# Hybrid transformer blocks, fp32, one core: a gate panel of HGRN ahead of the gated delta's scores, and the solver's `gd_x0` behind the panel of HGRN's values

## Chip, core and metric

The kernel runs on one core of a Trainium2 chip. The metric is the device time of one execution in microseconds. The kernel before takes 1782.95 us (median of three runs).

## What is computed

Two blocks follow one another on an input of 256 positions by 1024 channels, all in float32. The first has two layers of FFN, mixer, FFN; the second is one layer of retention, dilated attention, MLP and a gated embedding. The change is in the mixer of the first block, so it runs twice. The mixer projects the normed input with `w_in` and runs three parts side by side, HGRN2 (`hg_`), gated delta (`gd_`) and RG-LRU (`rg_`):

```python
def hybrid_mixer(h, lb, w_in, ...):
    proj = (h @ w_in)
    (hg_q, hg_f, hg_i, hg_g, gd_q, gd_k, gd_v, gd_z, gd_b, gd_a,
     rg_x, rg_gate) = jnp.split(proj, SPLIT_POINTS, axis=-1)
    o_hg = hgrn2_chunked(q, 1.0 - f, hg_i, jnp.log(f))
    o_hg = head_rmsnorm(o_hg, hg_norm_w) * jax.nn.silu(hg_g)
    o_gd = gated_delta_chunked(cq, ck, cv, g, beta)
    o_gd = head_rmsnorm(o_gd, gd_norm_w) * jax.nn.silu(gd_z)
    o_rg = rg_lru(xc, wr, br, wi, bi, lam) * jax.nn.gelu(rg_gate, approximate=True)
    return jnp.concatenate([o_hg, o_gd, o_rg], axis=-1) @ w_out

# inside gated_delta_chunked, for each chunk
    lower = jnp.where(strict, jnp.einsum('bhtd,bhsd->bhts', kb, ki) * decay, 0.0)
    sol = lax.linalg.triangular_solve(eye + lower, rhs, left_side=True, lower=True, unit_diagonal=True)
    scores = jnp.einsum('bhtd,bhsd->bhts', qi, ki) * decay
```

`hg_g` is columns 768 to 1023 of `w_in` (the gate panel that the change moves) and `hg_i` columns 512 to 767 (HGRN's values).

## The kernel before

All weights pass through the core once, in panels of 1 MB. SyncE loads a panel into one of three `raw` slots. ScalarE makes its high half `w_hi` (line 1526), VectorE the low half `w_lo` = raw - w_hi (line 2028), each with two slots, and TensorE multiplies high by high, high by low and low by high. A panel of 256 columns of `w_in` is 48 matmuls of 256 columns into one of three PSUM banks `colb` (c modulo 3), and ScalarE evacuates the bank with the activation of the panel (line 1636).

The order of all work is one list, `schedule`. The functions of `mixer` append panels (`cp`) and steps (`step`) to it, and each engine's program walks the whole list in that order, doing its own part of each entry. So moving one entry moves it on every engine. An entry has parts besides what it is named for:

- For ScalarE a panel entry first makes w_hi up to the next panel (`split_hi_to(p + 1)`), which waits for the raw data and for the end of the panel two before it; then it evacuates its own bank.
- For VectorE a panel entry makes w_lo up to the next panel (`split_lo_to(p + 1)`), which waits for that panel's w_hi. With `next_later` (the panel of hv) it goes only to its own. The steps in `AHEAD` (`spread` among them) also make w_lo one panel on.
- For TensorE a panel entry is its matmuls.

The steps around the change, with what each engine does: `spread` puts the gates on all partitions; its last part on ScalarE (line 1842) raises `gates_read`. `hg_exponents` n: VectorE builds differences of the cumulated log gates (lines 2389 and 2390), ScalarE takes their exponentials (line 1849). `gd_scores`: TensorE, once `gates_read` is there, makes 32 products k k' and k q' of 128x128 into the four `acc` banks; VectorE scales eq (2327), then for each of two chunks masks (2331), scales (2338) and adds the identity (2341), which raises `gd_x`, then makes sc (2343). `gd_x0`: TensorE multiplies the solver's first matrices by the identity, 32 small matmuls; ScalarE copies them out (1859) and resets a buffer (1853). `hg_first`: VectorE, two products (2396, 2397). `rg_end`: VectorE, the scan of RG-LRU and its gate (2316 to 2321). Then the solver's loop, i = 1 to 6: `gd_y` (TensorE; VectorE's masked copy at line 2352), `hg_level` (TensorE and VectorE) and `gd_z` (TensorE; ScalarE copies at 1879).

Line 917 is the helper through which nearly all matmuls go, so they are told apart by their tiles.

Of the kernel before, what the change touches and what calls it, by code (L numbers as in the profile page):

```python
# [26 lines left out]
PC = 256  # L27
# [87 lines left out]
def build(nc, ap, out, stop_at=None):  # L115
    ctx = ExitStack()
    with ctx:
# [57 lines left out]
        def view(at, *shape):  # L175
            n = int(np.prod(shape))
            v = arena[:, at:at + n]
            if len(shape) == 2:
                v = v.rearrange("p (a b) -> p a b", b=shape[1])
            if len(shape) == 3:  # L180
                v = v.rearrange("p (a b c) -> p a b c", b=shape[1], c=shape[2])
            return v
# [23 lines left out]
        hf, hq, hgate = view(A2, 2, T), view(A2 + 512, 2, T), view(A2 + 1024, 2, T)  # L206
# [74 lines left out]
        def panel(src, kt, ncols, kind, xop, ready, **more):  # L281
            nonlocal n_col, n_act, n_dve, n_row
            r = dict(p=len(panels), src=src, kt=kt, nc=ncols, kind=kind, xop=xop, ready=ready, **more)
            if kind != "row" and early[0]:
                n_scaled[0] += 1
                r.update(xop=g_op(early[1]["ops"]), ready=[], gained=count["fill"] if early[0] == EARLY else None, scaled=n_scaled[0],
                         norm=count["norm"], fill=early[1], half=EARLY - early[0])
                early[0] -= 1
                fresh[0] = True
            elif kind != "row":  # L290
                r["fresh"], fresh[0] = fresh[0], False
            if kind != "row":
                r["c"] = n_col
                n_col += 1
                if r["by"] == "act":
                    n_act += 1
                    r["n"] = n_act
                else:
                    n_dve += 1
                    r["n"] = n_dve  # L300
                bank_users.append((r["by"], r["n"]))
            else:
                n_row += 1
            panels.append(r)
            schedule.append(("panel", r))
            return r
# [33 lines left out]
        def step(name, **more):  # L340
            schedule.append((name, dict(panel=len(panels), nx=count["x"], op=len(ops), **more)))
# [21 lines left out]
        def pre_norm(gain, at):  # L363


            step("gained", gain=gain, at=at, n=count["fill"] + 1)
            n = norm_sum("x", "fill", gain=gain, at=at)
            f = fill(norm=n, gain=gain, at=at)
            return f

        def x_update(kind, **more):
            count["x"] += 1
            step("x_update", kind=kind, group=count["group"], first=0, **more)
            if kind in ("half", "whole"):
                acc_reader[0] = ("x_updated", 4 * count["x"])
            if kind == "post":
                count["normed"] += 1
                acc_reader[0] = ("acc_normed", 4 * count["normed"])

        def operand(src, ready):  # L380

            r = dict(r=len(ops), src=src, ready=ready)
            ops.append(r)
            return r
# [7 lines left out]
        def kpn(w):  # L392
            return w.rearrange("(k p) n -> p k n", p=P)

        def row_gemm_panel(w, i, r, first, last, base=None, woven=False, by_token=False):
            if r is not None:
                ready = [("op_ready", r["r"] + 1)]
                r["panel"] = len(panels)
                get = op_tiles(r)
            else:  # L400
                ready = base[0]
                get = (lambda kk, i=i: base[1](2 * i + kk))
            if first and acc_reader[0]:
                ready = ready + [acc_reader[0]]
            p = panel(kpn(w)[:, 2 * i:2 * i + 2, :], 2, D, "row", get, ready, first=first, last=last, woven=woven, by_token=by_token)
            if last:
                count["group"] += 1
            return p
# [51 lines left out]
        def mixer(l):  # L460
            f = pre_norm("norm_mix", KD * l)
            w = kpn(ap["w_in"][l])
            ready = [("u_ready", 4 * f)]

            def cp(c0, n, kind, evac, by="act", **more):
                return panel(w[:, :, c0:c0 + n], KD, n, kind, u_op, ready, by=by, evac=evac, **more)["n"]

            def y_operand(i, ready):
                r = operand(u32[:, 2 * i:2 * i + 2, :].rearrange("p a b -> p (a b)"), [ready])
                step("op_hi", r=r)  # L470
                step("op_lo", r=r)
                return r

            def gd_panel(i, **more):
                return cp(1024 + i * PC, PC, "A",
                          ("tap", gd_in[:, 2 * i:2 * i + 2, 3:], qkv[:, 2 * i:2 * i + 2, :], 48 * l + 36 + 2 * i), **more)


            b = cp(RGX0, PC, "A", ("copy", rg_in[:, :, 3:], 0))
            e = gd_panel(0)  # L480
            step("rg_conv", l=l, evac=b)
            for i in range(1, 6):
                n = gd_panel(i, split_first=i == 1)
                if i == 1:
                    cp(GATES0, P, "A", ("copy", gt[0], 0, 8), by="dve")
                    step("gate_rows", l=l)
                step("gd_conv", l=l, i=i - 1, evac=e)
                e = n
            cp(2560, PC, "A", ("silu", z[:, 0:2, :]))
            step("gd_conv", l=l, i=5, evac=e)  # L490
            step("gate_log", l=l)
            step("gate_cum", l=l)
            step("gd_ss", l=l)
            f = cp(256, PC, "A", ("sigmoid", hf))
            step("rg_gates", l=l)
            step("gate_copies", l=l)
            e = cp(0, PC, "A", ("silu", hq))
            step("hg_log", l=l, evac=f)
            step("rg_scan", l=l)
            step("spread", l=l)  # L500
            step("hg_cum", l=l, evac=e)
            for n in range(3):
                step("hg_exponents", l=l, n=n)
            d = cp(RGX0 + PC, PC, "A", ("gelu", rgate))
            step("gd_scores", l=l)
            cp(768, PC, "A", ("silu", hgate))
            step("gd_x0", l=l)
            step("hg_first", l=l)
            e = cp(512, PC, "B", ("copy", hv, 0), next_later=True)
            step("rg_end", l=l, evac=d)  # L510

            n = 0
            for i in range(1, 7):
                step("gd_y", l=l, i=i)
                for half in range(2):
                    if n < 9 and (half == 0 or i <= 3):
                        step("hg_level", l=l, n=n, evac=e)
                        n += 1
                    if half == 0:
                        step("gd_z", l=l, i=i)  # L520
                    if n <= 9 and (half == 0 or i <= 3) and n + 2 < 8:
                        step("hg_exponents", l=l, n=n + 2)
                if i == 1:
                    y_rg = operand(u32[:, 6:8, :].rearrange("p a b -> p (a b)"), [("rg_y", l + 1)])
                    step("op_hi", r=y_rg)
                if i == 4:
                    step("op_lo", r=y_rg)
            acc_reader[0] = ("gd_solved", 2 * l + 2)
            woven = row_gemm_panel(ap["w_out"][l], 3, y_rg, True, False, woven=True)
            step("hg_out", l=l, woven=woven)  # L530
            step("gd_chunks", l=l)
            y_hg = y_operand(0, ("hg_y", l + 1))
            step("gd_norm", l=l)
            row_gemm_panel(ap["w_out"][l], 0, y_hg, False, False)
            tail_c[l] = n_col
            ready = [("gd_orstd", 2 * l + 1)]
            step("gd_out", l=l, i=0)
            y_gd = y_operand(1, ("gd_out", 2 * l + 1))
            e = cp(2560 + PC, PC, "A", ("silu", z[:, 2:4, :]))
            step("gd_out", l=l, i=1, evac=e)  # L540
            row_gemm_panel(ap["w_out"][l], 1, y_gd, False, False)
            y_gd = y_operand(2, ("gd_out", 2 * l + 2))
            row_gemm_panel(ap["w_out"][l], 2, y_gd, False, True)
            x_update("whole")
# [2127 lines left out]
```

How the kernel before makes its waits and increments, by code:

```python
        def first_ready(eng, part, p, b):  # L732
            if b < 3:
                eng.wait_ge(sem(f"first_{part}"), 3 * p + b + 1)
            else:
                eng.wait_ge(sem(f"w_{part}_ready"), p + 1)
# [8 lines left out]
        def evacuated(eng, n):  # L746
            by, done = bank_users[n]
            eng.wait_ge(sem(f"{by}_evac"), done)
# [1 line left out]
        def col_bank_free(eng, n):  # L750
            evacuated(eng, n)
            both = [last_both[i] for i in (n, n + 1, n + 2) if i in last_both]
            if both:
                eng.wait_ge(sem("both_added"), both[-1])
# [1 line left out]
        def bank_done(eng, r, b):  # L757
            if b < 3:
                eng.wait_ge(sem("acc_bank"), 3 * (r["group"] - 1) + b + 1)
            else:
                eng.wait_ge(sem("panel_used"), r["panel"])
# [31 lines left out]
        @block.sync  # L794
# [4 lines left out]
            def load_quarter(b):  # L799
                dst = chunk_of(raw[:, 0, :], b).rearrange("p (k n) -> p k n", k=2)
                if b >= 2:
                    sp.wait_ge(sem(f"x_loaded{b - 2}"), 16)
                sp.dma_start(dst, panels[0]["src"][:, 2 * b:2 * b + 2, :]).then_inc(sem(FIRST_RAW[b][0]), 16)
# [8 lines left out]
                if what == "panel":  # L813
                    p = r["p"]
                    if p == 0:
                        continue
                    if p == 2:
                        sp.wait_ge(sem("first_hi"), 2)
                    if p == RAW_SLOTS:
                        sp.dma_start(cst[:, :], ap["constants"]).then_inc(sem("cst_loaded"), 16)
```

## Time and profile before

| | |
|---|---|
| time, median of 3 runs | 1782.95 us (1779.75 to 1783.29) |
| span of the profiled execution | 1778.3 us (its own time is not given beside its span) |
| TensorE busy | 1732.5 us, 97% |
| VectorE busy | 1136.7 us, 64% |
| ScalarE busy | 969.5 us, 55% |
| mean granted TensorE clock | 0.996 |
| chain that ended last | TensorE 82%, ScalarE 7%, VectorE 6% |

Busy shares are over the whole span. The FFNs, where TensorE is the only limit, take most of it; the mixer stretches, where three engines hand work to one another, lie from about 177 to 365 us and from about 719 to 907 us. In the rows of the trace "start us, us" are the start and the length of a group of instructions of one kind; the length of the last matmul contains its pipeline latency, so a group's end overlaps the start of the next. The bracket at the end is the idle time of the engine before the group and what ended it.

### The profile page before, as it was taken

Reading aid. Unit: us, or ns where it says so; the run is one execution under the profiler, and the core shown is the slowest. Engines: PE = TensorE matmul, PEld = TensorE weight load, DVE = VectorE, ACT = ScalarE, POOL = GpSimd, SP = SyncE. Lnnn points to the kernel's source line nnn. Section 1 sums busy time; section 2 is a strip of 40 time slices with the busy share of each in tenths; the row PEclk is TensorE's granted clock in tenths of the full one; section 3 lists DMA queues with packets and bytes.
Section 4 is the critical chain, followed back from the end, with each engine's and each line's share of the span. In section 5 each row is a group of like instructions: output and inputs, shape, how many; then the busy total and the mean of one; then the engine's idle time right before and its main releaser. Section 6 shows DMA issues by size and latency. Waiting matters only on the chain.

```text
span 1778.3 us, 30205 instructions
## 1 busy us (share of the span) xinstructions
PE 1732.5 (97%) x12990; PEld 1576.1 (89%) x12990; DVE 1136.7 (64%) x1344; ACT 969.5 (55%) x1107; POOL 107.9 (6%) x86
## 2 busy tenths in 40 slices
PE   9999999999999999999899999999999999999996
PEld 8888998898889888998898888989898879899996
DVE  6656788575567555798765556564465566775557
ACT  5544686564456444587664446544445464654445
POOL 1000001000000000001000000692000000000000
PEclk9999999999999999999999999999999999999999
DMA  8555562255655656562146565556255524455551
GB/s 279 166 191 189 157 186 73 73 169 187 196 188 163 199 181 207 157 189 96 55 152 199 183 196 160 176 192 205 90 167 189 165 69 165 158 180 190 189 173 41
DMA packets 206997, 290.81 MB, mean 164 GB/s; under 512 B 4656, under 2 KB 170672, under 8 KB 206736
## 3 DMA queue, kind: packets, MB, share of 16 engines
q1 hardware_dynamic: 206416, 287.11, 49.9%
q8 instruction: 103, 1.69, 0.4%
q0 software_dynamic: 448, 1.77, 0.3%
q14 instruction: 30, 0.25, 0.0%
HBM read 287.81 MB, written 1.05 MB: 162 GB/s over the span
## 4 chain that ended last, share of the span: by engine, by line
PE 82%; ACT 7%; DVE 6%; issue 2%; POOL 2%; DVEq 0%; ACTq 0%; POOLq 0%
PE colb L917 53%; PE acc L917 28%; ACT w_hi L1526 2%; DVE u L2126 2%; DVE w_lo L2028 1%; PE acc L1117 0%; DVE x L2164 0%; POOL arena L787 0%; DVE u L2163 0%; PE colb L1455 0%; ACT arena L1977 0%; ACT L1648 0%; ACT rstd L1652 0%; ACT L1636 0%; DVE arena L2269 0%
## 5 line engine op out<-in xcount | busy, mean ns | idle before, releaser
L2028 DVE TENSOR_TENSOR w_lo<-raw,w_hi 128x2048 fp32r<-128x2048 f32 x269 | 625.9, 2327 | 389.2 <-ACT w_hi L1526 388.5
L1526 ACT ACTIVATE w_hi<-raw 128x2048 fp32r<-128x2048 f32 x269 | 512.1, 1904 | 228.4 <-PE acc L917 178.8
L917 PE MATMUL colb<-u_both,w_hi 128*128 128x256 f32 (+1 forms) x3328 | 551.0, 321 | 0.6
L917 PEld LDWEIGHTS colb<-u_both,w_hi 128*128 128x128 f32 x3328 | 481.8, 190 | 48.2 <-ACT u_both L1751 2.8
L917 PE MATMUL colb<-u_both,w_lo 128*128 128x256 f32 x2240 | 291.3, 283 | 0.3 <-DVE w_lo L2028 0.3
L917 PEld LDWEIGHTS colb<-u_both,w_lo 128*128 128x128 f32 x2240 | 283.2, 192 | 6.1 <-DVE w_lo L2028 0.5
L917 PE MATMUL colb<-w_hi,u_both 128*128 128x512 f32 (+1 forms) x480 | 110.0, 378 | 0.3 <-ACT w_hi L1526 0.3
L917 PEld LDWEIGHTS colb<-w_hi,u_both 128*128 128x128 f32 x480 | 85.1, 188 | 16.8 <-ACT w_hi L1526 0.5
L917 PE MATMUL acc<-w_lo,op_hi 128*128 128x512 f32 x384 | 95.3, 390 | 3.2 <-DVE w_lo L2028 3.2
L917 PE MATMUL acc<-op_hi,w_hi 128*128 128x256 f32 x544 | 96.9, 286 | 0.9 <-ACT arena L1886 0.9
L917 PE MATMUL acc<-w_hi,op_hi 128*128 128x512 f32 x384 | 96.3, 392 | 0.1
L917 PE MATMUL acc<-op_hi,w_lo 128*128 128x256 f32 x544 | 95.6, 284 | 0.2
L917 PE MATMUL acc<-op_lo,w_hi 128*128 128x256 f32 x544 | 95.0, 283 | 0.0
L917 PE MATMUL acc<-w_hi,op_lo 128*128 128x512 f32 x384 | 94.8, 389 | 0.0
L917 PEld LDWEIGHTS acc<-w_lo,op_hi 128*128 128x128 f32 x384 | 71.8, 188 | 19.4 <-DVE w_lo L2028 4.6
L1578 ACT ACTIVATE act_t<-colb 128x512 f32<-128x512 f32 x36 | 21.5, 598 | 122.6 <-PE colb L917 122.6
L917 PEld LDWEIGHTS acc<-w_hi,op_lo 128*128 128x128 f32 x384 | 72.1, 188 | 15.0
L917 PEld LDWEIGHTS acc<-w_hi,op_hi 128*128 128x128 f32 x384 | 69.0, 189 | 12.6 <-ACT w_hi L1526 0.3
L917 PEld LDWEIGHTS acc<-op_hi,w_hi 128*128 128x128 f32 x544 | 78.6, 191 | 1.5 <-ACT arena L1886 1.2
L917 PEld LDWEIGHTS acc<-op_hi,w_lo 128*128 128x128 f32 x544 | 78.4, 192 | 0.7 <-DVE w_lo L2028 0.7
L917 PEld LDWEIGHTS acc<-op_lo,w_hi 128*128 128x128 f32 x544 | 78.5, 192 | 0.0
L917 PE MATMUL acc<-arena 64*64 64x64 f32 (+3 forms) x1448 | 67.6, 232 | 9.9 <-ACT small L1842 6.2
(321 smaller groups left out, 1839.0 us busy)
## 6 DMA issues: line engine op xcount, KB each, us to landing
raw<-w_in SPq DMA_DIRECT2D x78, 1024.0 KB, 5.1
raw<-ffn_up SPq DMA_DIRECT2D x44, 1024.0 KB, 5.3
raw<-ffn_down SPq DMA_DIRECT2D x44, 1024.0 KB, 4.9
raw<-ffn_gate SPq DMA_DIRECT2D x43, 1024.0 KB, 5.3
raw<-w_up SPq DMA_DIRECT2D x16, 1024.0 KB, 5.4
raw<-w_down SPq DMA_DIRECT2D x16, 1024.0 KB, 4.9
raw<-w_out SPq DMA_DIRECT2D x8, 1024.0 KB, 4.8
raw<-w_ret_out SPq DMA_DIRECT2D x8, 1024.0 KB, 4.9
```

Of the source, the lines that this page charges most:

```text
L917: return pe.matmul(o, a, b, start=start, stop=stop, skip_group_check=True)
L1526: act.activation(split_view(w_hi, r), raw[:, p % RAW_SLOTS, 0:r["kt"] * r["nc"]], ACT.Copy)\
L1578: act.activation(both_dst(r).rearrange("p (m t) -> p m t", t=T), colb4[:, r["banks"], T:2 * T], ACT.Copy)\
L2028: tt(split_view(w_lo, r), raw[:, p % RAW_SLOTS, 0:r["kt"] * r["nc"]], split_view(w_hi, r).bitcast(F32), ALU.subtract).then_inc(sem("w_lo_r ...
L2126: ins = stt(u32[:, kk, :], x[:, kk, :], c(r["gain"], r["at"] + kk), rstd[:, :], ALU.mult, ALU.mult)
```

## The change

Two entries of the mixer's list move. The gate panel (`cp(768, ...)`, hgate) goes in front of `gd_scores`, and `gd_x0` goes behind `hg_first` and the panel of HGRN's values (`cp(512, ...)`, hv). Nothing is added or taken away.

```diff
             d = cp(RGX0 + PC, PC, "A", ("gelu", rgate))
+            cp(768, PC, "A", ("silu", hgate))
             step("gd_scores", l=l)
-            cp(768, PC, "A", ("silu", hgate))
-            step("gd_x0", l=l)
             step("hg_first", l=l)
             e = cp(512, PC, "B", ("copy", hv, 0), next_later=True)
+            step("gd_x0", l=l)
             step("rg_end", l=l, evac=d)
```

## Rows read from the trace of the kernel before

**Rows 1.** The page's part 1: busy time, share of the span, instructions.

```profile
PE 1732.5 (97%) x12990; PEld 1576.1 (89%) x12990; DVE 1136.7 (64%) x1344; ACT 969.5 (55%) x1107; POOL 107.9 (6%) x86
```

**Rows 2.** TensorE's waits, whole span: us in total, times, longest us.

```profile
PE acc L917 <- ACT small L1842: 6.2, 2, 3.1
```

**Rows 3.** TensorE in order of time, layer 0.

```profile
279.87 5.47 PE L917 MATMUL acc<-arena 128*128 128x128 f32 x32 [3.09 <-ACT small L1842]
285.10 4.07 PE L917 MATMUL colb<-u_both,w_hi 128*128 128x256 f32 x32
...
291.01 1.15 PE L917 MATMUL acc<-cst,arena 64*64 64x64 f32 x32
292.09 4.10 PE L917 MATMUL colb<-w_hi,u_both 128*128 128x256 f32 x32
...
298.04 1.15 PE L917 MATMUL acc<-arena 64*64 64x64 f32 x32
299.12 0.71 PE L917 MATMUL colb<-sq 64*128 64x128 f32 x8
299.76 2.02 PE L917 MATMUL acc<-arena 64*64 64x64 f32 x61
```

**Rows 4.** The same in layer 1.

```profile
822.28 5.47 PE L917 MATMUL acc<-arena 128*128 128x128 f32 x32 [3.09 <-ACT small L1842]
...
842.17 2.02 PE L917 MATMUL acc<-arena 64*64 64x64 f32 x61
```

**Rows 5.** Windows of layer 0: length; busy (instructions) by engine; PEclk, DMA, GB/s.

```profile
281.00:282.00 1.00, 1.00 (x7) 1.00 (x6) 0.97 (x2) 0.00 (x0) 1.00 (x1) 0.50 0.00 0
284.00:285.10 1.10, 1.10 (x13) 1.10 (x12) 0.86 (x3) 1.04 (x3) 0.00 (x0) 1.00 0.00 0
...
276.80:299.76 22.96, 19.89 (x200) 19.37 (x201) 21.55 (x43) 12.90 (x18) 4.99 (x5) 0.93 0.24 80
299.76:345.00 45.24, 40.29 (x870) 36.92 (x869) 32.31 (x70) 25.95 (x48) 0.00 (x0) 1.00 0.14 52
345.00:365.00 20.00, 20.00 (x166) 19.93 (x165) 9.56 (x10) 10.98 (x11) 0.00 (x0) 1.00 0.43 130
```

**Rows 6.** VectorE in order of time, layer 0.

```profile
272.45 2.29 DVE L2028 TENSOR_TENSOR w_lo<-raw,w_hi 128x2048 fp32r<-128x2048 f32 x1 [2.19 <-ACT w_hi L1526]
...
284.01 0.68 DVE L2327 TENSOR_TENSOR arena<-arena 128x512 f32<-128x512 f32 x1
...
285.38 0.69 DVE L2331 TENSOR_TENSOR arena<-acc,arena 128x512 f32<-128x512 f32 x1 [0.48 <-PE acc L917]
...
288.22 0.68 DVE L2331 TENSOR_TENSOR arena<-acc,arena 128x512 f32<-128x512 f32 x1
...
293.22 2.29 DVE L2028 TENSOR_TENSOR w_lo<-raw,w_hi 128x2048 fp32r<-128x2048 f32 x1
295.43 0.42 DVE L2396 TENSOR_TENSOR sq<-sq,arena 128x256 f32<-128x256 f32 x1
...
299.30 0.71 DVE L2352 COPY_PREDICATED arena<-cst,acc 128x256 f32<-128x256 int32 x2
```

**Rows 7.** ScalarE in order of time, layer 0.

```profile
279.62 0.20 ACT L1842 ACTIVATE small<-small 128x4 f32<-128x4 f32 x1
282.78 1.97 ACT L1849 ACTIVATE sq<-sq 128x512 f32<-128x512 f32 x3 [2.96 <-DVE sq L2390]
284.77 1.28 ACT L1636 ACT_TABLE_LOAD   x1
286.06 0.60 ACT L1636 ACTIVATE arena<-colb 128x512 f32<-128x512 f32 x1
286.56 1.91 ACT L1526 ACTIVATE w_hi<-raw 128x2048 fp32r<-128x2048 f32 x1
...
293.10 1.91 ACT L1526 ACTIVATE w_hi<-raw 128x2048 fp32r<-128x2048 f32 x1
```

**Rows 8.** SyncE's DMA queue in order of time.

```profile
295.59 0.37 SPq L826 DMA_DIRECT2D raw<-w_in  x1
```

## The prediction

> **What bounds the kernel now.** I read the page's busy times first: TensorE is busy in 97% of the span [rows 1], so only its idle time, about 46 us, and matmuls that run slowly can be won, and any new idle time is lost at once. The list of TensorE's waits comes next: its largest entry is `gd_scores` waiting for line 1842, the last activation of `spread`, twice 3.1 us, once in each layer [rows 2]. Then I read the engines in order of time around that wait, in layer 0. TensorE ends the gelu panel at 276.78 (279.87 less the wait), sits idle for 3.09 us, computes the scores until 285.1, then hgate's panel, `gd_x0`, the panel of hv, `gd_y(1)`, `hg_level(0)`, and starts `gd_z(1)` at 299.76 [rows 3]. Layer 1 repeats it, shifted by 542.4 us [rows 4]. The windows show a second price of the wait: behind the gap the granted clock is 0.50, the lower level (1.2 GHz), and at 284.0 it is 1.00 again [rows 5]. Last come VectorE's and ScalarE's rows of the same stretch, since both halves of every weight panel are made there in program order [rows 6, 7].
>
> **Which wait ends last at the end of the stretch.** `gd_z(1)` needs VectorE's `gd_y` copy (line 2352, starts 299.30, the first of two done about 299.66), and TensorE is there at 299.76 [rows 3, 6]. The two engines arrive together: VectorE has no slack. It is without a break from 285.38 to 298.1 but for hundredths, and between 284.0 and the copy only 0.48 us is idle that waits for TensorE [rows 6]; of the 22.96 us from the end of the gelu panel to `gd_z(1)` it is busy 21.55 [rows 5]. So whatever TensorE gains must pass VectorE, and what VectorE loses moves `gd_z(1)`.
>
> **Part 1, hgate's panel in front of the scores.** Cost on TensorE: its duration does not change, 285.10 to 291.01, 5.91 us [rows 3]. It can start at 276.78: its high half was made in ScalarE's earlier split, its low half at 272.45 plus 2.29 = 274.74 [rows 6]. It ends at 276.78 + 5.91 = 282.69, after `gates_read` (279.82) [rows 7], so the 3.09 us wait is covered. The scores then follow a busy stretch. At the full clock 13 matmuls fit in 1.10 us, 85 ns each, at half clock 7 in 1.00 us, 143 ns [rows 5]; 32 x 85 ns = 2.7 us against 5.23 now. Scores: 282.7 to 285.4. Up to here TensorE is 3.09 + 2.5 = 5.6 us better per layer. The Trainium skill (TensorE: Matmul & The Clock Gate, What's actually happening) says that the throttled state is the default and that activity releases it; by that rule alone the full 5.6 us would stay, and the trace agrees that the slow matmuls lie behind the gap [rows 5].
>
> **What the moved panel step issues beside its matmuls.** In VectorE's list a panel step first makes the low half of the next panel's weights. hgate's step therefore makes w_lo of hv's panel. Before, this stood behind `gd_scores` (293.22, 2.29 us) [rows 6]; now it stands in front of it. It waits for w_hi of hv. ScalarE makes that in its own hgate step, and there nothing moves: ScalarE waits for the exponents until 282.78, loads a table at 284.77, evacuates gelu at 286.06 and makes w_hi from 286.56 for 1.91 us, done 288.47 [rows 7]. Nothing in that chain depends on the scores. So:
> - VectorE is free at 284.0 and waits until 288.5: a stall of about 4.4 us in place of the 0.48 us.
> - Queued behind that wait are all of `gd_scores` (eq, dlast, two masked products, sc), `hg_first`, `rg_end` and the `gd_y` copy.
> - w_lo from 288.5; the next instruction 2.21 us later (293.22 to 295.43), at 290.7. From 284.01 to 293.22 VectorE's `gd_scores` takes 9.21 us, less 0.48 idle = 8.73 [rows 6]. So `hg_first` starts at 299.44 instead of 295.43. From there to the copy is 3.87 us (295.43 to 299.30): copy at 303.3, first half done 303.7.
> The net is 4.49 - 0.48 = 4.0 us on VectorE per layer. The split itself is moved, not added.
>
> **Part 2, `gd_x0` behind hv's panel.** TensorE, free at 285.4, finds hv's w_hi ready at 288.5: a new wait of 3.05 us, in place of the old one. hv takes 292.09 to 298.04, 5.95 us [rows 3]: until 294.5; its w_lo (done 290.8) is early. `gd_x0` needs VectorE's two products: 290.7 + 0.9 + 2.84 = 294.5 and 297.3 (2.84 us is the distance of the two L2331 rows). It ends at 297.9 after a wait of 2.3 us, `gd_y(1)` waits for ScalarE's copy and for sc until 299.1 for its second half and ends at 299.65, `hg_level(0)` waits for `hg_first` (299.44 + 0.76 = 300.2) and ends at 300.9; then 2.8 us of idle until 303.7. Were the clock low again in hv's panel, its end would come at most 2.5 us later (what the low stretch cost the scores now), 297.0, still ahead of 297.3: covered by VectorE, at no cost. ScalarE's `gd_x0` copies now stand behind hv's evacuation, due at 295.1, so no cost either. ScalarE's next split (293.10 before, the woven panel) needs only hgate's matmuls and comes earlier, at about 290.3. No table load is added: gelu, silu and the copies keep their order.
>
> **DMA queue and GpSimd.** The load that waits for hv's w_lo (295.59) goes out at 290.8 instead, earlier [rows 8]; the panel it feeds comes only behind the solver's loop, so this is worth nothing. GpSimd's queue has none of the moved steps.
>
> **Sum.** `gd_z(1)` starts at 303.7 instead of 299.76: +3.95 us in layer 0 and, with the same rows, in layer 1 [rows 4]: +7.9 us. Does anything give it back? From 299.76 to 345 TensorE is busy 40.3 of 45.2 us [rows 5]; its short waits there are for ScalarE and VectorE, which are behind by the same 4 us, and then comes a stretch that is fully busy [rows 5]. I see nothing that absorbs it. Span 1778.3 + 7.9 = 1786.2. The median of the three runs is 4.65 us above the profiled span; the profiled execution's own time is not shown, so I add the same: 1790.9 us, 0.44% slower.
>
> The unshown term is the clock behind the new idle time. Bounds per layer: 0, or 2.5 us, the price of the low stretch on the scores. The low stretches of before follow one whole gap of 3.09 us [rows 2, 5]; the gap before `gd_z(1)` is 2.8 us with short work and short gaps ahead of it. That is near, but what follows are 64x64 matmuls that share the time with copies on the other engines. I take 0 and keep up to 2.5 for the range. Below nothing: TensorE's clock can't make VectorE's chain shorter, so no gain beyond 0 is in this term.
>
> **Rivals.**
> - A, faster: VectorE's chain turns out not to hold `gd_z(1)` and the full 5.6 us per layer stays: 1782.95 - 11.2 = 1771.8. It decides if w_hi of hv is ready by the time VectorE ends the exponents (284.1 instead of 288.5). Against it: two ScalarE instructions and a table load stand in front of it, and the copy at 299.30 is already level with TensorE. 5%.
> - B, the change does not do what I read: the low half of hv stays behind VectorE's `gd_scores`. Then it is ready at 295.5; hv's panel starts at 288.5, waits for it from 292.5, ends 297.5; `gd_x0`, `gd_y(1)`, `hg_level(0)` follow (1.1 + 1.1 + 0.65, and short waits) and `gd_z(1)` starts at 300.5: +0.7 us a layer, 1784.4. The same band holds a partial absorption of the delay later in the mixer, up to 1786.5. 10%.
> - C, slower than forecast: the clock falls behind the gap at 303.7. Up to 2 x 2.5: 1791 to 1796, middle 1793.5. It decides if the gaps between 295 and 303.7 count like the one gap of 3.09 us. By the skill's account of the clock gate (same page, HAM oscillation — how this bites in real kernels), waits of TensorE that recur bring the low clock back each time; that is this rival. The trace shows it for the long gap alone. 20%.
> - Forecast, 1786.5 to 1792.5, likeliest 1790.9: 65%.
>
> **How the numbers follow.** A measurement of this kernel tells about 0.2%, 3.6 us, from no change; the three runs differ by 3.5 us. Slower by more than that (above 1786.5) takes the forecast and C: 0.85. Same: B, 0.09. Faster: A and a little for what I have not seen, 0.06. The range leaves out A, most of B and the far end of C: 1786.5 to 1795.
>
> **What would show it.** The largest wait of TensorE is no longer line 1842 but w_hi of hv (about 3 us) and the `gd_y` copy of line 2352 (about 2.8 us), beside a wait of 2.3 us in `gd_x0` for line 2341. VectorE has a wait of 4.4 us on line 1526 at 284 and starts line 2327 at 290.7. The scores take 2.7 us at clock 1.00. Wrong would be: line 2327 still at 284.0 (B), a copy of line 2352 by 299.5 (A), or a clock under 1.00 behind 303.7 (C).

## The result and the profile after

The changed kernel takes 1790.79 us (median of 5 runs, 1790.13 to 1794.04). Five runs of the kernel before beside it have their median at 1780.16 (1779.75 to 1783.29). The ratio is 1.0059, with a 95% interval of 1.0048 to 1.0070: slower, by 10.6 us. The execution that was profiled took 1790.13 us with a span of 1788.2, thus 1.9 us around its span; its span is 9.9 us over that of before.

TensorE in order of time in the changed kernel, layer 0 and the end of the same stretch in layer 1:

```profile
276.74 4.00 PE L917 MATMUL colb<-u_both,w_hi 128*128 128x256 f32 x32
280.58 2.08 PE L917 MATMUL colb<-u_both,w_lo 128*128 128x256 f32 x16
282.50 3.73 PE L917 MATMUL acc<-arena 128*128 128x128 f32 x32
288.74 4.06 PE L917 MATMUL colb<-w_hi,u_both 128*128 128x256 f32 x32 [2.51 <-issue]
292.64 2.08 PE L917 MATMUL colb<-w_lo,u_both 128*128 128x256 f32 x16
294.66 0.68 PE L917 MATMUL acc<-cst,arena 64*64 64x64 f32 x16
297.50 1.12 PE L917 MATMUL acc<-cst,arena 64*64 64x64 f32 x16 [2.16 <-DVE arena L2341]
298.40 1.99 PE L917 MATMUL acc<-arena 64*64 64x64 f32 x32
300.43 0.84 PE L917 MATMUL colb<-sq 64*128 64x128 f32 x8
303.83 3.33 PE L917 MATMUL acc<-arena 64*64 64x64 f32 x61 [2.56 <-DVE arena L2352]
...
850.67 3.37 PE L917 MATMUL acc<-arena 64*64 64x64 f32 x61 [2.69 <-DVE arena L2352]
```

Beside [rows 3]: the wait of 3.09 us in front of the scores is gone, and three others have come, 2.51 us in front of hv's panel, 2.16 in `gd_x0` and 2.56 in front of `gd_z(1)`, which starts at 303.83 instead of 299.76. The 2.51 us are put down to "issue"; ScalarE's rows below show that w_hi of hv ends there. The page's list of TensorE's waits (total, times, longest) has the entry of [rows 2] no more. At its head stand:

```profile
PE acc L917 <- DVE arena L2352: 6.0, 4, 2.7
PE colb L917 <- issue: 5.0, 2, 2.5
PE acc L917 <- DVE w_lo L2028: 3.2, 3, 2.8
PE colb L917 <- ACT op_hi L1671: 3.0, 6, 1.0
PE acc L917 <- DVE arena L2341: 2.8, 2, 2.2
```

VectorE in order of time, as [rows 6]:

```profile
288.68 2.29 DVE L2028 TENSOR_TENSOR w_lo<-raw,w_hi 128x2048 fp32r<-128x2048 f32 x1 [4.40 <-ACT w_hi L1526]
290.88 0.69 DVE L2327 TENSOR_TENSOR arena<-arena 128x512 f32<-128x512 f32 x1
...
299.52 0.42 DVE L2396 TENSOR_TENSOR sq<-sq,arena 128x256 f32<-128x256 f32 x1
...
303.39 0.71 DVE L2352 COPY_PREDICATED arena<-cst,acc 128x256 f32<-128x256 int32 x2
```

The low half of hv stands in front of VectorE's `gd_scores` and waits 4.40 us for the high half, which ScalarE makes where it did before [rows 7]:

```profile
286.25 0.60 ACT L1636 ACTIVATE arena<-colb 128x512 f32<-128x512 f32 x1
286.74 1.90 ACT L1526 ACTIVATE w_hi<-raw 128x2048 fp32r<-128x2048 f32 x1
```

Windows of the changed kernel (columns as in [rows 5]): from hgate's panel through the scores, behind the start of `gd_z(1)` in layer 0, and the same in layer 1:

```profile
276.74:286.00 9.26, 9.26 (x82) 9.26 (x80) 7.50 (x15) 4.79 (x8) 5.23 (x5) 1.00 0.26 107
303.70:307.20 3.50, 3.37 (x69) 3.37 (x71) 3.46 (x12) 0.90 (x2) 0.00 (x0) 0.56 0.02 5
850.20:853.70 3.50, 3.02 (x56) 3.03 (x58) 3.46 (x12) 0.90 (x2) 0.00 (x0) 0.51 0.00 0
```

The clock stays at 1.00 (2.4 GHz) through the scores, where it was 0.50 at 281 [rows 5], and is now low in `gd_z(1)`, behind the waits. There 61 matmuls take 3.33 us that took 2.02 [rows 3].

**Where the 9.9 us lie.** The norm's matmuls near the end of each mixer, before and after:

```profile
343.62 1.99 PE L917 MATMUL colb<-sq,one_row 128*128 128x256 f32 x8 [0.24 <-ACT sq L1917]
885.16 1.99 PE L917 MATMUL colb<-sq,one_row 128*128 128x256 f32 x8 [0.24 <-ACT sq L1917]
```

```profile
348.17 1.99 PE L917 MATMUL colb<-sq,one_row 128*128 128x256 f32 x8 [0.24 <-ACT sq L1917]
895.01 1.99 PE L917 MATMUL colb<-sq,one_row 128*128 128x256 f32 x8 [0.24 <-ACT sq L1917]
```

Layer 0 is behind by 348.17 - 343.62 = 4.55 us, both layers by 9.85; the FFNs and the second block add nothing. When `gd_z(1)` starts, layer 0 is 4.07 us behind; 0.13 of them are there before the stretch, since ScalarE's line 1842 starts at 279.75 instead of 279.62 [rows 7]. In layer 1 `gd_z(1)` starts 8.5 us behind [rows 4], 3.95 more than the 4.55. The rows with which `gd_z(3)` starts, two rounds of the solver later, in both layers, before and after:

```profile
309.54 2.02 PE L917 MATMUL acc<-arena 64*64 64x64 f32 x61 [0.23 <-DVE arena L2352]
851.95 2.02 PE L917 MATMUL acc<-arena 64*64 64x64 f32 x61 [0.36 <-DVE arena L2352]
```

```profile
314.96 2.02 PE L917 MATMUL acc<-arena 64*64 64x64 f32 x61 [0.36 <-DVE arena L2352]
861.80 2.02 PE L917 MATMUL acc<-arena 64*64 64x64 f32 x61 [0.36 <-DVE arena L2352]
```

From `gd_z(1)` to there the kernel before takes 9.78 us in both layers and the changed one 11.13, so the low stretch costs 1.35 us in each. In layer 0 the difference at the norm is smaller, because the trace of before has an idle time later in its loop, put down to "issue", that neither its own layer 1 nor the changed kernel has:

```profile
317.34 0.85 PE L917 MATMUL acc<-arena 64*64 64x64 f32 x22 [1.13 <-issue]
```

It makes the rest of that layer, from `gd_z(3)` to the norm, 34.08 us instead of 33.21. So layer 0 is 4.07 + 1.35 - 0.87 = 4.55 us, and layer 1 is 3.95 + 1.35 = 5.30.

### The profile page after: what moved, and what is told of

Its sections match the earlier page's. It is cut to its first block, busy times and chain, and to the rows that moved or that the text cites. A ratio compares the mean times of both kernels' runs of the same rounds, so it can differ in the third digit from the quotient of the medians.

```text
span 1788.2 us, 30205 instructions
## 1 busy us (share of the span) xinstructions
PE 1734.7 (97%) x12990; PEld 1578.5 (88%) x12990; DVE 1136.8 (64%) x1344; ACT 969.5 (54%) x1107; POOL 107.9 (6%) x86
## 4 chain that ended last, share of the span: by engine, by line
PE 80%; DVE 8%; ACT 8%; issue 3%; POOL 2%; DVEq 0%; ACTq 0%; POOLq 0%
PE colb L917 52%; PE acc L917 27%; ACT w_hi L1526 3%; DVE u L2126 2%; DVE w_lo L2028 1%; PE acc L1117 0%; ACT L1636 0%; DVE x L2164 0%; ACT L1648 0%; POOL arena L787 0%; DVE u L2163 0%; PE colb L1455 0%; ACT arena L1977 0%; DVE arena L2338 0%; ACT rstd L1652 0%
```

## The experiments

**Theory:** a panel entry makes the next panel's low half on VectorE. Moved in front of `gd_scores`, it puts a wait for ScalarE in front of VectorE's chain to the `gd_y` copy, which had no slack. **Rivals:** TensorE's own order of panels costs the time, or the low clock does.

Each kernel was timed beside the kernel before, whose median moved between 1780.2 and 1782.1 from one group of runs to the next. So kernels of different groups are compared by their ratios; 0.1% is 1.8 us.

| kernel | median us | ratio | 95% interval |
|---|---|---|---|
| the change | 1790.79 | 1.0059 | 1.0048 to 1.0070 |
| gate panel alone moved | 1797.12 | 1.0084 | 1.0071 to 1.0096 |
| `gd_x0` alone moved | 1784.07 | 1.0015 | 1.0006 to 1.0024 |
| change, low split back | 1788.39 | 1.0035 | 1.0021 to 1.0049 |
| change, early high split | 1784.14 | 1.0012 | 1.0004 to 1.0021 |
| the same, wait filled, ten | 1781.49 | 0.9998 | 0.9989 to 1.0006 |
| the same, wait filled, twenty | 1784.05 | 1.0019 | 1.0010 to 1.0028 |
| change, wait filled, ten | 1791.04 | 1.0053 | 1.0040 to 1.0065 |
| change, wait filled, twenty | 1793.13 | 1.0069 | 1.0055 to 1.0082 |
| change, zeros on ScalarE | 1784.68 | 1.0016 | 1.0007 to 1.0025 |
| change, early high split, zeros on ScalarE | 1776.29 | 0.9974 | 0.9964 to 0.9984 |
| before, zeros on ScalarE | 1780.18 | 0.9997 | 0.9989 to 1.0006 |
| before, early high split, zeros on ScalarE | 1781.44 | 0.9999 | 0.9990 to 1.0008 |

### Each half of the change alone

```diff
+            cp(768, PC, "A", ("silu", hgate))
             step("gd_scores", l=l)
-            cp(768, PC, "A", ("silu", hgate))
             step("gd_x0", l=l)
             step("hg_first", l=l)
             e = cp(512, PC, "B", ("copy", hv, 0), next_later=True)
```

> The kernel before with hgate's panel alone moved in front of gd_scores; gd_x0 stays directly behind the scores and in front of hv's panel. Theory: the wait of VectorE is the same as in the change (its list is the same), and TensorE has no panel to put behind the scores: it waits from 286.1 for VectorE's first products (294.6) and second (297.5), then hv to 304, gd_y(1) 305.1, hg_level(0) 305.8, gd_z(1) at 305.9: 6.1 us a layer over the kernel before, 12 us, and up to 3 us more for a low clock behind the 8.4 us gap: 1792 to 1796. So the second move would be a gain of 4 to 5 us on top of the first. Rival (the second move makes the loss): below 1785.

Measured 1797.12, as a time 1.1 us above the range. Over the kernel before of its own group it is 15 us, the upper end of the 12 and up to 3 more that were worked out. TensorE:

```profile
294.59 1.12 PE L917 MATMUL acc<-cst,arena 64*64 64x64 f32 x16 [8.43 <-DVE arena L2341]
297.42 1.12 PE L917 MATMUL acc<-cst,arena 64*64 64x64 f32 x16 [1.72 <-DVE arena L2341]
```

and its window behind that wait:

```profile
294.60:300.50 5.90, 4.18 (x41) 3.88 (x42) 5.53 (x13) 2.29 (x5) 0.00 (x0) 0.50 0.17 56
```

The loss is there with the gate's panel alone moved. TensorE stands 8.43 us in front of the first product of the solver (line 2341), then runs 5.9 us at 0.50. The second move puts hv's panel into that wait and wins 0.25%, 4.5 us, of it back.

The other half:

```diff
-            step("gd_x0", l=l)
             step("hg_first", l=l)
             e = cp(512, PC, "B", ("copy", hv, 0), next_later=True)
+            step("gd_x0", l=l)
```

> The kernel before with gd_x0 alone moved behind hv's panel; hgate's panel stays behind the scores. Theory: VectorE's list is that of the kernel before, so no new wait on it; hv's panel starts 1.1 us earlier and waits 0.5 us for its low half, gd_x0 ends at 298.6, gd_y(1) waits for ScalarE's copy and ends 299.65, gd_z(1) at 300.3: 0.5 us a layer, 1780 to 1782, no difference that can be measured. The 3.09 us wait and the low clock behind it stay. Rival (gd_x0 behind hv costs by itself, since its copies come late): 1785 or more.

1784.07, ratio 1.0015: 2.7 us slower, where 1 us and no measurable difference were expected and the rival began at 5. Its `gd_z(1)` starts at 300.77 in a trace whose scores start 0.2 us later than before: 0.8 us a layer, where 0.5 was worked out. The last microsecond stays open: the profiled execution, 1786.54, is one of the slower of this kernel, and its scores in layer 1 take 6.52 us instead of 5.47. This half is a small loss by itself, and not the source of the ten.

### The low split back behind `gd_scores`

```diff
-            cp(768, PC, "A", ("silu", hgate))
+            cp(768, PC, "A", ("silu", hgate), next_later=True)
```

> The changed kernel with one thing undone: hgate's panel entry no longer makes the low half of hv's panel, so on VectorE w_lo of hv stands behind gd_scores and hg_first again. Theory (the low split in front of VectorE's gd_scores makes the loss): the 4.4 us wait of VectorE at 284 is gone, the scores' products start when TensorE ends the scores, about 286.1. But hv's panel, started at 288.7, now waits for its low half: hg_first ends at 294.7, w_lo at 297.0, hv at 299.0, gd_x0 300.1, gd_y(1) 301.1, hg_level(0) 301.8: gd_z(1) at about 301.8, 2.0 us a layer behind the kernel before and 2.0 ahead of the change; 1784 to 1787 with a low clock behind the 4.3 us wait. Rival (the order of the two panels' matmuls and the clock make the loss, whatever VectorE does): no difference from the change, about 1790.

1788.39, ratio 1.0035: 6.2 us behind the kernel before of its group, within the 4 to 7 of the theory, though as a time above its 1787, and 2 to 4 us ahead of the change (2.4 by the medians, 4.3 by the ratios). The trace has the wait where it was worked out, in hv's panel, but `gd_z(1)` 2 us later than the 301.8 that were expected:

```profile
297.27 3.68 PE L917 MATMUL colb<-w_lo,u_both 128*128 128x256 f32 x16 [4.33 <-DVE w_lo L2028]
...
303.77 2.02 PE L917 MATMUL acc<-arena 64*64 64x64 f32 x61
```

```profile
297.20:300.90 3.70, 3.63 (x18) 3.45 (x18) 2.86 (x6) 0.00 (x0) 0.00 (x0) 0.54 0.69 188
```

Behind a wait of 4.33 us the clock is low, and the 16 matmuls with w_lo take 3.68 us instead of 2.08. With that, `gd_z(1)` starts as late as in the change (303.77 and 303.83), but itself runs at full clock: to `gd_z(3)` it takes 9.77 us, not 11.13. That, about 1.35 us a layer, is most of what this kernel is faster by. So the two places for the low half are both bad: in front, VectorE waits for ScalarE; behind, TensorE waits for VectorE. Taking away VectorE's wait for w_hi in this way gives back less than half of the loss.

### The high split early

ScalarE has nothing to do from 279.9 to 282.8 [rows 7]. There it can make w_hi of hv:

```diff
             def hg_exponents(r):
                 ...
+                if n == 0:
+                    split_hi_to(r["panel"] + 2)
                 act.wait_ge(sem("hg_de"), 8 * l + n + 1)
```

> The changed kernel, and ScalarE makes w_hi of hv before the exponents, in the 3 us in which it waits for VectorE (279.9 to 282.8), instead of behind gelu's evacuation. Theory (what costs is that VectorE waits for w_hi of hv in front of its gd_scores): the wait of 4.4 us is gone, w_lo of hv is made at 284.0 to 286.3, TensorE starts hv directly behind the scores at 286.1, the sequence of VectorE ends as in the kernel before or 0.4 us earlier: gd_z(1) at about 299.4, no low clock: 1779 to 1780.5 where the kernel before has 1780.2, thus 10 us faster than the change. Rival A of the prediction (without that wait the whole 5.6 us a layer come in): 1769 to 1771. Rival (the order of TensorE's panels makes the loss): 1788 to 1791.

1784.14, ratio 1.0012: 0.47% or 8.4 us ahead of the change, but 2 us behind the kernel before, where the theory had it level or ahead. VectorE's wait is gone, TensorE runs from hgate through hv without a stop, and most of what it gained stands in one wait:

```profile
279.82 1.91 ACT L1526 ACTIVATE w_hi<-raw 128x2048 fp32r<-128x2048 f32 x1
```

```profile
282.48 3.73 PE L917 MATMUL acc<-arena 128*128 128x128 f32 x32
285.96 4.08 PE L917 MATMUL colb<-w_hi,u_both 128*128 128x256 f32 x32
...
299.33 2.68 PE L917 MATMUL acc<-arena 64*64 64x64 f32 x61 [2.69 <-DVE arena L2354]
```

(Line 2354 is line 2352 of before.) `gd_z(1)` starts 0.43 us earlier than before, as worked out. Rival A of the prediction, that the whole gain comes in once VectorE no longer waits, has fallen: VectorE's work is the bound, not only its wait. What was missed is the clock:

```profile
299.30:302.70 3.40, 3.37 (x81) 3.37 (x83) 3.37 (x11) 1.42 (x4) 0.00 (x0) 0.67 0.02 5
```

In the kernel before the low stretch lay in the scores, ahead of a start of `gd_z(1)` for which VectorE was only just ready. Now it lies in `gd_z(1)`, where ScalarE and VectorE wait for each result.

### The wait in front of `gd_z(1)` filled

```diff
                 for j in range(NT):
+                    if i == 1 and j == 0:
+                        for _ in range(20):
+                            mm(bank[0][:, 4 * HP:4 * HP + P], ones, ones)
                     if i < 6:
                         pe.wait_ge(sem("gd_y_copied"), 10 * l + 2 * (i - 1) + j + 1)
```

> The changed kernel with 20 matmuls of ones by ones (128x128, about 2.2 us together) on TensorE behind hg_level(0), into the half of the bank that gd_z(1) overwrites; their result is not used. They fill the 2.6 us wait in front of gd_z(1) and take nothing from another engine. Theory (of the change's 10 us, 4 a layer are VectorE's later copy and the rest, 1 a layer, is gd_z(1) running at the lower clock behind this wait): gd_z(1) starts at 303.8 as in the change and takes 2.0 instead of 3.3 us, no low stretch at 304: 1.3 us a layer less at most, since the low stretch does not fall there in every execution: 1787.5 to 1790, against 1791 for the change. Rival (the low clock costs nothing there, since the other engines pace the loop): 1791.

> The changed kernel with the early high split and with the same 20 idle matmuls in front of gd_z(1). Theory: with the high split early, gd_z(1) starts at 299.3, 0.4 us before the kernel before, and what lost it 2 us against that kernel is the low clock behind the 2.7 us wait; filled, it loses only what it gains: 1781 to 1782.5, the level of the kernel before, 2 us less than without the filling. Rival (the wait is not what brings the clock down, or it costs nothing): 1784.

Both missed, since the filling was too long: each product of ones is two instructions, and 20 take 4.7 us, not 2.2. In the second kernel:

```profile
297.79 4.73 PE L917 MATMUL acc<-one_row 128*128 128x128 f32 x40
302.45 2.02 PE L917 MATMUL acc<-arena 64*64 64x64 f32 x61
```

`gd_z(1)` runs at full clock, but 2 us late. The times (1793.13 and 1784.05) decide nothing. With ten products, which take 2.5 us:

> The changed kernel with half as many idle matmuls in front of gd_z(1), ten, since twenty took 4.7 us and ended 2 us behind VectorE's copy. Ten take about 2.4 us and fit in the wait of 2.6 us. Theory (the low clock in gd_z(1) costs up to 1.3 us a layer): gd_z(1) starts when VectorE's copy is there, as in the change, and takes 2.0 instead of 3.3 us: 1788.5 to 1790 against 1791. Rival (the low clock there costs nothing): 1791. If the clock falls from the earlier waits of the stretch, the gain is smaller and a low stretch lies between 295 and 304.

> The changed kernel with the early high split and ten idle matmuls (2.4 us) in the 2.7 us wait in front of gd_z(1). Twenty had kept the clock up in the profiled run but ended 2 us too late. Theory (what sets the early split 2 to 3 us behind the kernel before is the low clock behind this wait, since its gd_z(1) starts 0.4 us earlier): 1780 to 1782, 2 to 3 us less than without the filling, with no low stretch behind 299. Rival (the low clock costs nothing or falls anyway): 1784.

With the early split the filling is worth 0.14%, 2.5 us (1784.14 to 1781.49, ratios 1.0012 and 0.9998, intervals that overlap only at their ends), as expected. Its window from the filling into `gd_z(1)`:

```profile
299.00:303.00 4.00, 3.74 (x84) 3.55 (x84) 3.68 (x11) 0.74 (x2) 0.00 (x0) 1.00 0.02 4
```

So the low clock behind this wait costs about 1.2 us a layer. The traces agree: from `gd_z(1)` to `gd_z(3)` the early split takes 10.50 us in layer 0 and 11.31 in layer 1, and the filled kernel 9.77 in layer 0. Without the low stretch the early split is level with the kernel before. On the change itself ten products brought nothing that the times can tell (1791.04; 1.0053 against 1.0059). In layer 0 of its trace the low stretch had moved ahead of the filling, behind the waits in front of hv and in `gd_x0`:

```profile
299.50:303.00 3.50, 3.46 (x50) 3.08 (x46) 3.25 (x8) 0.99 (x3) 0.00 (x0) 0.51 0.00 0
```

The case that this expectation names last came about in layer 0. There the low clock cost almost nothing: `gd_z(1)` starts 21.42 us behind the start of the scores (21.33 in the change), runs at full clock, and `gd_z(3)` follows 9.77 us later. From the scores to the norm this trace takes 64.40 us in layer 0 and 64.55 in layer 1, and the change 65.67 and 65.66: 2.4 us less together, 0.13%, which the intervals of the two ratios are too wide to tell. So what the low clock costs in the change is shown by traces of one execution each, not by the times.

### VectorE relieved

The four memsets between VectorE's `gd_scores` and its copy go to ScalarE, which idles there. The edit is shown shortened: left out are the signal `rg_y`, which moves to the product in front, and VectorE's new wait for `hat_clear` in a later `hg_level`.

```diff
 # VectorE, gd_scores and rg_end
-                    dve.memset(xt[halves[1], j, :]...[:, :, 0:HP], 0.0)
-                dve.memset(hat[halves[1], :, :, 0:HP], 0.0)
-                dve.memset(hatc, 0.0).then_inc(sem("rg_y"), 1)
 # ScalarE, a new rg_end
+                for j in range(NT):
+                    act.activation(xt[hi, j, :]...[:, :, 0:HP], bc(k("half_ident", 0, HP)[hi], 1, 4), ACT.Copy, scale=0.0)
+                act.wait_ge(sem("rg_y"), l + 1)
+                act.activation(hat[hi]...[:, :, 0:HP], bc(k("half_ident", 0, HP)[hi], 1, 8), ACT.Copy, scale=0.0)
+                act.activation(hatc..., bc(k("half_ident", 0, HP), 1, 8), ACT.Copy, scale=0.0).then_inc(sem("hat_clear"), 1)
```

> The changed kernel with the early high split, and VectorE's four memsets per layer between gd_scores and the gd_y copy (xt twice, hat, hatc) made by ScalarE, which waits there. VectorE's sequence is then 1.1 + 0.58 = 1.7 us shorter. Theory (VectorE's sequence sets the start of gd_z(1)): gd_z(1) at 297.6 instead of 299.3, the wait in front of it about 1.0 instead of 2.7 us, and no low clock behind it: 2.1 us a layer ahead of the kernel before: 1777 to 1779 where that has 1781.8. Rival (something else, ScalarE's copies or the matmuls, sets it): 1782 to 1784.

1776.29, ratio 0.9974: faster than both, by 4.7 us against the kernel before and by 0.85%, 15 us, against the change, at the good end of the difference that was expected. TensorE and the window behind its wait, layer 0:

```profile
296.93 2.02 PE L917 MATMUL acc<-arena 64*64 64x64 f32 x61 [1.46 <-DVE arena L2363]
```

```profile
296.90:300.40 3.50, 3.47 (x126) 3.48 (x130) 3.47 (x11) 3.14 (x7) 0.00 (x0) 1.00 0.02 5
```

The copy (now line 2363) starts 12.44 us after hv's low half (284.00 to 296.44), where it was 14.72 with the early split alone (284.18 to 298.90): 2.28 us less. The memsets' own durations are only 1.5 of them (0.27 twice and 0.48 twice); the rest are the gaps at their ends. `gd_z(1)` is 2.83 us ahead of the kernel before, and in layer 0 the clock is 1.00 behind the shorter wait. In layer 1 the same wait is followed by the low clock:

```profile
835.71 3.23 PE L917 MATMUL acc<-arena 64*64 64x64 f32 x61 [1.46 <-DVE arena L2363]
```

```profile
835.70:839.20 3.50, 3.49 (x73) 3.49 (x75) 3.46 (x11) 1.90 (x5) 0.00 (x0) 0.56 0.00 0
```

`gd_z(3)` follows 11.04 us behind `gd_z(1)` there and 9.77 in layer 0. So "no low clock behind it" held in one layer of this execution, and about 1.3 us is still lost in the other.

The same two edits apart and in the old order:

> The changed kernel as it is, with VectorE's four memsets on ScalarE and no early high split. Theory: VectorE's wait of 4.4 us stays, its sequence behind it is 1.7 us shorter, so gd_z(1) starts at 302.1 instead of 303.8: 1.7 us a layer less, 1787 to 1788, and less where the shorter wait also keeps the clock up: down to 1785.5. Against the 1776.3 of both edits together that gives the early high split 9 to 11 us. Rival (the memsets on ScalarE are the whole gain of the two edits): 1777.

> The kernel before, its order untouched, with only the four memsets on ScalarE. Theory: there TensorE itself arrives at gd_z(1) at 299.76, behind the 3.09 us wait and the scores at the lower clock, so a shorter sequence of VectorE brings nothing at gd_z(1); the low half of hv comes 0.6 us earlier and is not waited for: 1781 to 1782, no difference. Rival (VectorE alone sets the stretch in the kernel before too): 1778.5.

> The kernel before in its own order, with both edits that made the changed order fast: ScalarE's high split of hv before the exponents and the four memsets on ScalarE. Theory (the changed order is worth something only when VectorE is relieved, and the relief only in the changed order): TensorE still waits 3.09 us for line 1842 and computes the scores at the lower clock, gd_z(1) starts when TensorE is there, as in the kernel before: 1779.5 to 1781, no difference. Rival (the two edits are the whole gain and the order doesn't matter): 1776.

The memsets alone take the change from a ratio of 1.0059 to 1.0016, 7.7 us, where 3 to 5.5 were expected: in that trace `gd_z(1)` starts 2.2 us earlier, not 1.7, and runs at clock 1.00 in layer 0 (2.02 us), though not in layer 1 (3.23). The early high split on top of that is worth 0.42%, 7.5 us, a little under the 9 to 11 expected. In the old order neither the memsets (0.9997) nor both edits (0.9999) bring anything. In the last kernel TensorE keeps its old wait and VectorE has slack instead:

```profile
279.96 5.47 PE L917 MATMUL acc<-arena 128*128 128x128 f32 x32 [3.08 <-ACT small L1842]
...
299.86 2.02 PE L917 MATMUL acc<-arena 64*64 64x64 f32 x61
```

```profile
298.86 0.92 DVE L2363 COPY_PREDICATED arena<-cst,acc 128x256 f32<-128x256 int32 x2 [1.65 <-PE acc L917]
```

So order and relief pay only together: the relief makes VectorE ready earlier, the order lets TensorE be there too. Whether the relieved kernel needs both moves or only one was not run.

## Why the prediction was right, and where not

- **What bounds the stretch.** Right. TensorE and VectorE met at `gd_z(1)` with no slack on either; each single relief gained nothing (0.9999 with VectorE relieved, 1.0012 with TensorE's wait removed), both together did.
- **Part 1.** Right in kind: hgate from 276.74, the 3.09 us wait covered, the scores at clock 1.00. Wrong in size: the scores take 3.5 us, not 2.7 (with the early high split hv's panel follows 3.48 us behind their start). The step that failed is the 85 ns each, counted from 13 matmuls in 1.10 us of one window; over all 32 it is 109 ns. A window also counts the matmuls that only reach into it: half a microsecond of the changed kernel's scores shows 7, where 109 ns each makes 4.6. So 4.8 us a layer were gained up to there, not 5.6. It cost the sum nothing, because VectorE sets the end.
- **VectorE's wait.** Right within 0.2 us: a wait of 4.4 us forecast and 4.40 measured, line 2327 at 290.88 (290.7), `hg_first` at 299.52 (299.44), the copy at 303.39 (303.3). The wait for the high half is the cause, as making it early showed (8.4 us), together with VectorE's plain work behind it.
- **Part 2.** Right: waits of 2.51 (3.05 forecast, less the longer scores), 2.16 (2.3) and 2.56 us (2.8). Covered, as said, was a late hv: in layer 1 its high part runs at the lower clock, 5.55 us instead of 4.06, and the wait in `gd_x0` only shrinks:

```profile
835.58 5.55 PE L917 MATMUL colb<-w_hi,u_both 128*128 128x256 f32 x32 [2.50 <-issue]
...
844.34 0.68 PE L917 MATMUL acc<-cst,arena 64*64 64x64 f32 x16 [0.68 <-DVE arena L2341]
```

- **The sum.** +3.95 us a layer forecast, 4.07 and 3.95 measured at `gd_z(1)`, and 3.94 and 3.95 without the 0.13 us from before the stretch. Nothing in the changed kernel gave it back later.
- **The clock term.** Wrong: taken as 0, measured 1.35 us in each layer. The bound of 2.5 held it, though it was too large by the same 85 ns: the low stretch cost the scores 5.23 - 3.48 = 1.75 us. The reason given for 0, that these matmuls share the time with copies, had it the wrong way round: the copies wait for them (in layer 0 VectorE's next `gd_y` copy 0.89 us, ScalarE's 0.80). Rival C happened beside the forecast, not instead of it.
- **The time.** 1790.9 forecast, 1790.79 measured, but that is closer than the reasoning deserves. The forecast was 7.9 us (0.44%) slower, the measured difference is 10.6 us (0.59%). The base of three runs, 1782.95, was 2.8 us above the median of five, and it made up for the clock term (2.7 us): luck, not reasoning. The 4.65 us taken for what lies around the span were too much as well: for the changed kernel's profiled execution they are 1.9.
- **Rival A** fell with the early high split: its condition was met, and the gain did not come. Its condition should have been the end of VectorE's work, not the end of its wait.
- **Rival B** fell by the order of VectorE's rows. As an experiment its place of the split cost 0.35%, not 0.08%: the price left out that VectorE's products then wait for the scores, that in the edit `hg_first` too stands in front of the low half (w_lo is done at about 297.2, not 295.5), and the low clock behind a wait of 4.3 us.

## What to carry to other kernels

An entry of a common list that is moved takes all its side work with it; look on each engine at what the entry issues for its neighbours, here the next panel's split, before counting what the named work gains. When two engines arrive together at a join, a relief of one is worth nothing (0.12% lost here) until the other is relieved too; then the two relieve each other (0.26% won). Where a gain turns into a wait of some microseconds, look at what runs behind it: if that is what others wait for, the low clock costs there what it did not cost in its old place.

## What the runs showed of the hardware

- TensorE's clock is at 0.50 to 0.67 in the windows behind the longer waits (2.56, 2.69 and 4.33 us) and at 0.50 behind one of 8.43 us. Behind a wait of 1.46 us it stays at 1.00 in layer 0 and is 0.56 in layer 1 of the same execution (the kernel with the early high split and the zeros on ScalarE), so the length of the last wait alone does not decide it. With short work between them, two or three waits near one another (2.5, 2.2 and 2.6 us) are followed by low stretches that can lie at any of them: in the change in `gd_z(1)` and in layer 1 also in hv's panel, with ten filling matmuls in `gd_y(1)` (32 matmuls in 2.20 us against 1.28 with the zeros on ScalarE).
- What the low clock costs depends on who waits behind it: in `gd_y(1)`, ahead of a start that VectorE sets, at most 0.09 us; in `gd_z(1)` 1.35 us.
- A 128x128 product of ones costs TensorE 0.12 us for each of its two instructions (20 in 2.5 us).
- Four memsets whose rows add up to 1.5 us freed 2.28 us of VectorE: in front of each stands a gap of 0.1 to 0.2 us, where without it the next instruction starts 0.08 us before the row of the one in front ends (with the early split the memset of line 2322 starts at 297.86 behind a row that ends at 297.69; without the memsets the copy starts at 296.44 behind a row that ends at 296.52).
